# One fp32 transformer pair on one core: short vectors laid out as columns, x turned, the first w_ada sums moved ahead, and ScalarE copying both turned maps

## The reference, cut to what matters

```python
def first_block(x, c, ...):
    mod = silu(c) @ w_ada + b_ada              # 2048 -> 6 x 2048
    shift_a, scale_a, gate_a, shift_f, scale_f, gate_f = split(mod, 6)
    h = rms_norm(x, g_attn_pre) * (1 + scale_a) + shift_a
    proj = h @ w_in                            # 2048 -> 5456
    ...                                        # differential and indexed sparse attention
    x = x + gate_a * rms_norm(concat(diff_out, dsa_out) @ w_o, g_attn_post)
    h = rms_norm(x, g_ffn_pre) * (1 + scale_f) + shift_f
    x = x + gate_f * rms_norm((silu(h @ w_gate) * (h @ w_up)) @ w_down, g_ffn_post)

def second_block(x, ...):
    ...                                        # norm, w_in_2, 16 heads of MLA, a gated convolution, w_out_2
```

## Time and profile before

| what | before |
|---|---|
| median of 3 runs | 2403.71 us (2403.37 to 2404.49) |
| the profiled execution, its own time | 2403.83 us |
| its span from first to last instruction | 2402.5 us |
| TensorE busy, share of the span | 2288.5 us, 95% |
| VectorE busy | 1400.4 us, 58% |
| ScalarE busy | 1065.3 us, 44% |
| bytes moved | 505.69 MB, mean 210 GB/s |

### The profile page before, as it was taken

How to read it: one execution, slowest core, us unless ns; L and a number is a source line. 1 busy time by engine, 2 the same in 40 slices (tenths; PEclk the granted TensorE clock), 3 DMA queues, 4 the chain that set the end, 5 groups by cost and what they waited for, 6 DMA issues and landing times.

```text
span 2402.5 us, 26312 instructions
## 1 busy us (share of the span) xinstructions
PE 2288.5 (95%) x10768; PEld 1858.3 (77%) x10768; DVE 1400.4 (58%) x1903; ACT 1065.3 (44%) x1471; POOL 0.7 (0%) x5
## 2 busy tenths in 40 slices
PE   4899989889999999999998999999999999999998
PEld 2676767777888888888887878888888888888886
DVE  1459999795775464554456554545544554554554
ACT  2333544444444444434444555555444444444443
POOL 0000000000000000000000000000000000000000
PEclk7999999998999999999999999999999999999999
DMA  7888678593786675556553744444565555555553
GB/s 295 332 321 297 228 263 305 196 357 123 272 281 219 202 253 190 180 194 195 187 193 118 237 149 154 149 154 153 193 193 193 186 184 193 191 191 195 180 188 140
DMA packets 255455, 505.69 MB, mean 210 GB/s; under 512 B 9077, under 2 KB 19662, under 8 KB 254182
## 3 DMA queue, kind: packets, MB, share of 16 engines
q1 hardware_dynamic: 255334, 504.00, 62.2%
HBM read 499.77 MB, written 4.19 MB: 210 GB/s over the span
## 4 chain that ended last, share of the span: by engine, by line
PE 86%; DVE 7%; ACT 3%; DMA 2%; issue 1%; SPq 0%; DVEq 0%; ACTq 0%
PE bank L595 27%; PE bank L597 26%; PE bank L596 26%; DVE wlo L1674 2%; PE bank L611 2%; DMA raw<-in_w_in_dram 2%; DVE acc L1655 1%; PE bank L679 1%; ACT whi L1062 1%; DMA raw<-in_w_ada_dram 1%; PE bank L549 1%; PE bank L619 1%; DVE x L1726 0%; PE bank L702 0%; PE bank L531 0%
## 5 line engine op out<-in xcount | busy, mean ns | idle before, releaser
L1674 DVE TENSOR_TENSOR wlo<-raw,whi 128x1024 fp32r<-128x1024 f32 (+2 forms) x760 | 912.8, 1205 | 871.9 <-ACT whi L1062 870.2
L1062 ACT ACTIVATE whi<-raw 128x1024 fp32r<-128x1024 f32 (+2 forms) x760 | 789.9, 1044 | 1037.9 <-PE bank L597 917.5
L595 PE MATMUL bank<-whi,Ahi 128*128 128x512 f32 (+2 forms) x2304 | 910.8, 395 | 33.6 <-DVE wlo L1674 22.2
L596 PE MATMUL bank<-wlo,Ahi 128*128 128x512 f32 (+2 forms) x2304 | 896.6, 389 | 0.0
L597 PE MATMUL bank<-whi,Alo 128*128 128x512 f32 (+2 forms) x2304 | 896.4, 389 | 0.0
L595 PEld LDWEIGHTS bank<-whi,Ahi 128*128 128x128 f32 x2304 | 437.3, 190 | 132.9 <-DVE wlo L1674 31.9
L597 PEld LDWEIGHTS bank<-whi,Alo 128*128 128x128 f32 x2304 | 437.2, 190 | 90.2
L596 PEld LDWEIGHTS bank<-wlo,Ahi 128*128 128x128 f32 x2304 | 437.9, 190 | 83.4
L1655 DVE SCALAR_TENSOR_TENSOR acc<-raw,cs,acc 128x512 f32<-128x512 f32 x224 | 157.2, 745 | 0.1
L595 PE MATMUL bank<-whi,Fhi 128*128 128x512 f32 x352 | 137.6, 391 | 0.0
L597 PE MATMUL bank<-whi,Flo 128*128 128x512 f32 x352 | 137.1, 389 | 0.0
(11 more groups left out here) (291 smaller groups left out, 1344.3 us busy)
## 6 DMA issues: line engine op xcount, KB each, us to landing
raw<-in_w_in_dram SPq DMA_DIRECT2D x156, 1024.0 KB, 5.0
raw<-in_w_ada_dram SPq DMA_DIRECT2D x96, 1024.0 KB, 6.8
raw<-in_w_gate_dram SPq DMA_DIRECT2D x44, 1024.0 KB, 5.1
raw<-in_w_up_dram SPq DMA_DIRECT2D x44, 1024.0 KB, 5.1
raw<-in_w_down_dram SPq DMA_DIRECT2D x44, 1024.0 KB, 5.0
raw<-in_w_o_dram SPq DMA_DIRECT2D x16, 1024.0 KB, 6.7
raw<-in_w_o_mla_dram SPq DMA_DIRECT2D x16, 1024.0 KB, 4.9
raw<-in_w_o_conv_dram SPq DMA_DIRECT2D x16, 1024.0 KB, 4.9
```

The costliest lines, as they stand in the source:

```text
L595: pe.matmul(o, a_hi, w_hi, start=beg, stop=False)
L596: pe.matmul(o, a_hi, w_lo, start=False, stop=False)
L1062: act.activation(m.whi[:, i % NHL, :, 0:n], m.raw[:, c % NRAW, 2 * h:2 * h + 2, 0:n], ACT.Copy).then_inc(m.s_hi, 1)
L1674: dve.tensor_tensor(m.wlo[:, i % NHL, :, 0:n], m.raw[:, c % NRAW, 2 * h:2 * h + 2, 0:n], m.whi[:, i % NHL, :, 0:n].bitcast(F32), ALU.subtr ...
```

## The change

1. Short vectors, b_ada, positions, lambdas and x are laid out on the host: `columns` (128 x 121), `bias_columns` (128 x 96), `positions_both`, `lambdas`, and `x_turned` (columns of x on the partitions, 128 x 16 x 256). No arithmetic is done there. The ten small loads at the head become one; positions and lambdas become two loads that follow the ninth chunk.
2. x comes turned, so the mean squares are made over the partitions: ScalarE squares two halves, VectorE adds eight blocks of each (`red`), TensorE multiplies by ones, ScalarE takes the root, VectorE the reciprocal (`rstdT`). `turn_quarter` falls out of the first four quarters. VectorE makes `x * gs * rstdT` (`first_scale`), ScalarE adds the shift and rounds, VectorE makes the low part in one fused instruction (`first_shift`).
3. `first_scale` needs only the scale sums. They are made after the third chunk of a round, the shift's after the fourth. For the first quarter ScalarE's copies (`gather`) go ahead of the high parts of w_in, and the scale's sums stand among the products of the second group.
4. x in its plain form is loaded later, in four pieces, into the same space.
5. In sparse attention and MLA ScalarE copies both turned maps.

```diff
-    sp.dma_start(m.const[:, :], A["consts"]).then_inc(m.s_const, 16)
-    for r0, n, src in ((R_C, 16, A["c"][0]), ... (R_SUB, 1, A["g_diff_sub"][0])):
-        sp.dma_start(m.rows[r0:r0 + n, :], src.rearrange("(r n) -> r n", n=P)).then_inc(m.s_rows, 16)
...
+    sp.dma_start(m.cols[:, :], A["columns"]).then_inc(m.s_cols, 16)
+    load_chunk(0)
+    sp.dma_start(m.const[:, :], A["consts"]).then_inc(m.s_const, 16)
+    load_chunk(1)
+    for h in range(2):
+        sp.dma_start(m.xT[:, 8 * h:8 * h + 8, :], A["x_turned"][:, 8 * h:8 * h + 8, :]).then_inc(m.s_xT[h], 16)
+    load_chunk(2)
+    sp.dma_start(m.bT[:, :], A["bias_columns"]).then_inc(m.s_bT, 16)
+    for c in range(3, NRAW):
         load_chunk(c)
...
+        if c == LIN[0][0]:
+            sp.dma_start(m.pos[:, :], A["positions_both"]).then_inc(m.s_pos, 16)
+            sp.dma_start(m.lraw[:, :, :].rearrange("p a d -> p (a d)"),
+                         A["lambdas"].broadcast_to([P, 256])).then_inc(m.s_lamin, 16)
+        if c in at_x:
+            tb, h = divmod(at_x.index(c), 2)
+            need.wait_ge(m.s_shlo, 8)
+            cols = slice(1024 * h, 1024 * h + 1024)
+            sp.dma_start(x[:, tb, cols], A["x"][0, tb * P:tb * P + P, cols]).then_inc(m.s_x, 16)
```

TensorE:

```diff
+    def beside(idx, j):
+
+        if (idx, j) == (1, 0):
+            need.wait_ge(m.s_const, 16)
+            k.use(4)
+            for h in range(2):
+                need.wait_ge(m.s_red, h + 1)
+                ins = pe.matmul(m.bank[4][:, 0:S], m.ones, m.red[:, h, :], start=(h == 0), stop=(h == 1))
+            ins.then_inc(m.filled[4], 1)
+        if (idx, j) == (1, 2):
+            ada_columns(0)
...
-    ada_products(0)
-    first_operand(0)
+    ada_products(0, beside)
+    ada_columns(1)
     for q, cg in WIN_ITEMS[:3 * len(W_IN_FIRST)]:
         first_part(q, cg)
+        if cg == W_IN_FIRST[2]:
+            ada_columns(2 * q + 2)
         if cg == W_IN_FIRST[3]:
-            first_operand(q + 1)
+            ada_columns(2 * q + 3)
```

ScalarE (its squares, its shift, and both maps):

```diff
+    for h, o in enumerate((m.sq[:, :, :], m.tmpA[:, :, :, :].rearrange("p a k t -> p (a k) t"))):
+        need.wait_ge(m.s_xT[h], 16)
+        act.activation(o, m.xT[:, 8 * h:8 * h + 8, :], ACT.Square).then_inc(m.s_sq, 1)
+    warm_sqrt()
+    need.wait_ge(m.filled[4], k.use(4))
+    act.activation(m.rms[:, :], m.bank[4][:, 0:S], ACT.Sqrt, bias=m.eps[:, :], scale=1.0 / D).then_inc(m.freed[4], 1)
...
+                ins = act.activation(m.Ahi[:, kb, :], m.tmpA[:, q % 2, kk, :], ACT.Identity, bias=m.modT[:, kb:kb + 1])
...
     gather(0)
+    gather(1)
+    k.split_to(UNIT_AT[LIN[1]])
     first_operand(0)
...
-            copy_out(ln.ET[:, 0:384], b0, ex[0], m.bank[b0][:, 0:384])
+            for mm, b in enumerate(ln.bank[0:nm]):
+                copy_out(ln.ET[:, 384 * mm:384 * mm + 384], b, ex[mm], m.bank[b][:, 0:384])
...
-        copy_out(ln.ET[:, 0:384], 4, ex[0], m.bank[4][:, 0:384])
+        for mm in range(2):
+            copy_out(ln.ET[:, 384 * mm:384 * mm + 384], 4 + mm, ex[mm], m.bank[4 + mm][:, 0:384])
```

VectorE:

```diff
+        dve.tensor_reduce(m.red[:, h, :], i.rearrange("p k t -> p t k"), AX_X, ALU.add).then_inc(m.s_red, 1)
+    need.wait_ge(m.freed[4], k.use(4))
+    rstd_at = v.up(dve.reciprocal(m.rstdT[:, :], m.rms[:, :]))
...
+    def first_scale(q):
+
+        k.use(6)
+        mod(ADA_ON_PE[2 * q], 6, k.use(6))
...
+            ins = dve.scalar_tensor_tensor(out=m.tmpA[:, q % 2, kk, :], in0=m.xT[:, kb, :], scalar=m.gs[:, kb:kb + 1],
+                                           in1=m.rstdT[:, :], op0=ALU.mult, op1=ALU.mult)
...
+    def first_shift(q):
+
+        k.use(7)
+        mod(ADA_ON_PE[2 * q + 1], 7, k.use(7))
+        if q == 0:
+            k.split_to(UNIT_AT[LIN[1]])
...
+                ins = dve.scalar_tensor_tensor(out=m.Alo[:, kb, :], in0=m.tmpA[:, q % 2, kk, :],
+                                               scalar=m.modT[:, kb:kb + 1], in1=m.Ahi[:, kb, :].bitcast(F32),
+                                               op0=ALU.add, op1=ALU.subtract)
...
     for q, cg in WIN_ITEMS[:3 * len(W_IN_FIRST)]:
         first_part(q, cg)
         if cg == W_IN_FIRST[2]:
-            gather(q + 1)
+            first_scale(q + 1)
         if cg == W_IN_FIRST[3]:
-            first_operand(q + 1)
+            first_shift(q + 1)
         if (q, cg) == WIN_ITEMS[2]:
             tables()
...
-            if nm == 2:
-                need.wait_ge(m.filled[b1], ex[1])
-                dve.tensor_copy(ln.ET[:, 384:768], m.bank[b1][:, 0:384]).then_inc(m.freed[b1], 1)
```

More of the change, by code:

```diff
@@ L419, in __init__ @@
         after_P1 = shelf.top
-        self.rows = sb("rows", [P, P])
-        self.brows = sb("brows", [96, P])
         self.pos = sb("pos", [P, 4], I32)
@@ L536, in ada_take, with ada_products @@
             ins.then_inc(m.filled[b], 1)
-    def ada_products(c):
+    def ada_products(c, beside=None):
         while c < len(PLAN) and PLAN[c][0] == "ada" and c not in ADA_NO:
@@ L552, in ada_products @@
             c += 1
+            if beside:
+                beside(ADA_ON_PE.index(g), j)
     def ada_columns(idx):
@@ L1779, in shifted @@
             ins.then_inc(m.freed[b], 1)
-            if early:
-                low(j)
-        if not early:
-            low(0)
-            low(1)
-    def gather(q):
-        for idx in (2 * q, 2 * q + 1):
-            k.use(6 + idx % 2)
-    def first_operand(q):
-        for idx in (2 * q, 2 * q + 1):
-            b = 6 + idx % 2
-            mod(ADA_ON_PE[idx], b, k.use(b))
-        released(mod_at[4 + q], mod_at[q])
+            ks = slice(4 * q + 2 * j, 4 * q + 2 * j + 2)
+            need.wait_ge(m.s_shhi, base + 2 * q + j + 1)
+            dve.tensor_tensor(m.Alo[:, ks, :], tmp[:, q % 2, 2 * j:2 * j + 2, :], m.Ahi[:, ks, :].bitcast(F32),
+                              ALU.subtract).then_inc(m.s_shlo, 1)
+    def first_scale(q):
+        k.use(6)
+        mod(ADA_ON_PE[2 * q], 6, k.use(6))
+        released(mod_at[4 + q])
         ks = slice(4 * q, 4 * q + 4)
@@ L1798, in first_operand @@
         settle()
-        shifted(m.tmpA, q, 0, 0, False)
+        need.wait_ge(m.s_red, 2)
+        need.wait_ge(m.s_v, rstd_at)
+        if q > 1:
+            need.wait_ge(m.s_shlo, 2 * q - 2)
+        for kk in range(4):
+            kb = 4 * q + kk
+            ins = dve.scalar_tensor_tensor(out=m.tmpA[:, q % 2, kk, :], in0=m.xT[:, kb, :], scalar=m.gs[:, kb:kb + 1],
+                                           in1=m.rstdT[:, :], op0=ALU.mult, op1=ALU.mult)
+            if kk % 2 == 0:
+                v.up(ins)
+            else:
+                ins.then_inc(m.s_t, 1)
+    def first_shift(q):
[3 more added lines that the diff above has]
+            k.split_to(UNIT_AT[LIN[1]])
+        released(mod_at[q])
+        need.wait_ge(m.s_t, 2 * q + 2)
+        settle()
+        for j in range(2):
+            need.wait_ge(m.s_shhi, 2 * q + j + 1)
+            for kk in (2 * j, 2 * j + 1):
+                kb = 4 * q + kk
+                ins = dve.scalar_tensor_tensor(out=m.Alo[:, kb, :], in0=m.tmpA[:, q % 2, kk, :],
+                                               scalar=m.modT[:, kb:kb + 1], in1=m.Ahi[:, kb, :].bitcast(F32),
+                                               op0=ALU.add, op1=ALU.subtract)
+                if kk % 2 == 0:
+                    v.up(ins)
+            ins.then_inc(m.s_shlo, 1)
     part_at = {}
@@ L2136, in vector_program @@
     released(*y_at)
+    need.wait_ge(m.s_x, 64)
     for tb in range(2):
@@ L2550, in constants, with laid_out, rows @@
     return c
-_INS = ["x", "c", "positions", "w_ada", "b_ada", "g_attn_pre", "g_attn_post", "g_ffn_pre", "g_ffn_post", "w_in",
-        "lambda_q1", "lambda_k1", "lambda_q2", "lambda_k2", "g_diff_sub", "w_o", "w_gate", "w_up", "w_down",
-        "positions_2", "pre_norm_g_2", "w_in_2", "q_a_norm_g_2", "w_q_b_2", "kv_a_norm_g_2", "w_kv_b_2", "conv_w_2",
-        "w_o_mla_2", "w_o_conv_2", "w_out_2", "post_norm_g_2"]
+_INS = ["x", "w_ada", "b_ada", "g_attn_post", "g_ffn_post", "w_in", "w_o", "w_gate", "w_up", "w_down", "w_in_2",
+        "w_q_b_2", "w_kv_b_2", "w_o_mla_2", "w_o_conv_2", "w_out_2", "post_norm_g_2"]
+def laid_out(inputs):
+    def rows(name):
+        return np.asarray(inputs[name]).reshape(-1, P)
+    columns = ("c", "g_attn_pre", "g_ffn_pre", "pre_norm_g_2", "q_a_norm_g_2", "kv_a_norm_g_2", "conv_w_2", "g_diff_sub")
+    return {
+        "columns": np.concatenate([rows(n) for n in columns]).T,
+        "bias_columns": rows("b_ada").T,
+        "positions_both": np.concatenate([rows(n) for n in ("positions", "positions_2")]).T,
+        "lambdas": np.concatenate([np.asarray(inputs[n]) for n in ("lambda_q1", "lambda_k1", "lambda_q2", "lambda_k2")],
+                                  axis=1),
+        "x_turned": np.asarray(inputs["x"])[0].T.reshape(KD, P, S).transpose(1, 0, 2),
+        "consts": constants(),
+    }
 def kernel(**inputs):
@@ L2564 @@
     arrays, aps = {}, {}
-    for name in [*_INS, "consts"]:
```

(3 more changed lines are left out.)

136 lines of the change are left out of this document (46 added, 90 removed).

## The result

The changed kernel took **2381.95 us** (median of 4, 2381.28 to 2383.45), the kernel before, beside it, 2403.72 us (2403.37 to 2404.49): a ratio of 0.991, with an interval of [0.9893, 0.9927]. The forecast was 2382.0 us. The sum behind it was right in its two large terms and wrong in a smaller one, the rounds. That the two times agree so closely is luck: the same kernel taken again gave 2384.33 us.

A forecast was written before the change was run, and what follows sets the result against it. TensorE, busy 95% of the span, was taken as the bound, so a change counts only where it waits. Terms -10.0 - 2.8 - 1.2 - 1.0 - 6.7 = -21.7 from 2403.83 gave about 2382 us, range 2376 to 2393.

The forecast's parts named there:

- the rounds: Four rounds over quarters of w_in, 48.75 to about 177 us: net -1.2 us, bounds -5.3 and +3.
- The stream of loads: Kernel start: first w_ada chunk issued earlier, six small loads moved behind the ninth chunk; -10.0 us, bounds -7.1 and -10.8.
- The hole: Between w_ada's fifth and sixth chunk, behind six small loads: 7.1 us more than one chunk, forecast to close.
- From the last chunk to the first matmul: Start, last w_ada chunk to w_in's first matmul: 6.1 us instead of 8.84, -2.8 us, bounds -1.5 and -3.4.
- The reductions: Start, VectorE's two reductions of x's squares: 2.2 us each at 1.0 ns an element, 5.5 us spare before TensorE wants them.
- its point of 2.3 times: Strided-reductions rival at the start: beyond 2.3 times slower, each extra us holds TensorE's sixth chunk; 2416 us at ten times, chance 0.03.
- That stall: Rounds, before w_in's fifth chunk: TensorE waits 4.9 us for VectorE behind the rotation tables, 4.1 more than before.
- the third round ending some 14 us earlier: Sign that would show the forecast: the end of the third w_in round comes some 14 us earlier than before.
- The rival "loads set the rounds": Rounds wait for loads throughout, so only the stream's 10.0 us survives of the early terms: 2386 us, chance 0.12.
- Sparse attention: Before 470 us: four copies of 0.55 us move from VectorE to ScalarE; -1.0 us, bounds 0 and -2.2.
- MLA: MLA stage, 1380 to 1720 us: ScalarE's second copy lets TensorE go on 0.95 us earlier, seven times; -6.7 us.
- x read twice: Near 250 us: x loaded again in four 512 KB pieces, 1.3 us each; costs 0, bound +5.1.

The follow-up runs named there:

- the kernel with 16 matmuls more a round: Changed kernel plus 16 matmuls of 128x128 on the identity, results unused, in each of its first three rounds: 2388.91 us, ratio 0.9941.
- the first profile: First profiled execution of the unedited changed kernel, compared with the kernel before: 2383.45 us; the median of its runs was 2381.95 us.
- the five profiles with the changed kernel's rounds: Changed kernel twice, the two with MLA's or sparse attention's second copy back on VectorE, and one with two waits filled: rounds 124.2 to 128.5 us.
- the copies alone: Kernel before with only ScalarE copying both turned maps in sparse attention and MLA: 2393.57 us, ratio 0.9958.

## Why the prediction was right, step by step

- **The stream of loads, -10.0 us: right** (-9.65 at the eighth chunk's products). The hole did close. What made it I had left open; the runs put 4.2 us on the lambdas and 2.0 on the positions. Not all of it lasts: the first w_in chunk lands 9.6 us earlier than before (32.03 against 41.67), the second only 7.2 (44.76 against 51.92; 7.0 to 8.8 in the nine other profiles with the same order of loads). The new loads of positions and lambdas, which the forecast had put at nothing, stand right behind the first and cost 1.0 us there (0.7 to 2.0); where the rest goes was not looked into.
- **From the last chunk to the first matmul, 6.1 us forecast: right in size** (5.51; 5.5 to 7.0 in the other profiles with the same code and loads up to there). One cause was not in the working: before, TensorE stood 8.58 us ahead of the sixth chunk and its products ran at a granted clock of 0.50 up to the eighth. With a gap put back there by the old small loads, the changed code takes 8.3 us from the eighth chunk's landing too (33.71 to 40.90 from its products, all at 0.50), against 5.6 without and 8.9 before. So the new path is 3.3 us shorter where the clock stays up and 0.6 where it is down: part of this term's 2.8 us hangs on a condition that the forecast did not name.
- **The reductions, 2.2 us each: mis-sized.** They took 3.67, a factor of 1.67, and 2.9 us of the 5.5 spare were used up. The direction had been named as a rival, and its point of 2.3 times was not reached. The same shape read side by side, in the kernel with 16 matmuls more a round, took 2.28 us:

```profile
L2462 DVE TENSOR_REDUCE sg<-sg 128x256 f32<-128x2048 f32 x1 | 2.3, 2275 | 0.0
```

  So the forecast's 1.0 ns an element is nearly right for neighbours (1.1), and with steps of 1 KB it is 1.8. The Trainium skill, "SBUF — State Buffer", section "Door 1: The DMA port swizzle", says that an access that crosses to a new 16-byte line pays a penalty; this pair of rows agrees in direction. That the step between 16-byte lines is the cause, and not some other property of the step, was not tried.
- **The rounds, -1.2 us: the step that failed.** They gave 3.8 us back in the first profile. Over the five profiles with the changed kernel's rounds they are 126.0 us on average, against 124.7 and 121.7 in two profiles with the old rounds: some 2.8 us given back. The error was to credit the turning of x with its full 5.3 us of TensorE time, as if only the wait at the tables stood against it. That stall was right (5.39 us, 4.9 forecast). But the other waits of the rounds end 2.39 us after a load lands, whatever TensorE did before. With less work TensorE was idle longer, 16.8 us on average (14.4 to 18.3) instead of 11.2 and 11.1, which is 5.6 more where the forecast had 4.1, and its busy time fell by 2.9 us instead of 5.3, as the mean granted clock was 0.90 to 0.93 against 0.93 and 0.96. Of work put back, less than half shows (5 of 11 us). The sign named for this, the third round ending some 14 us earlier, did not come in the first profile: it is 9.2 us at unit 28, and 13.0 in the second. The rival "loads set the rounds" had the mechanism for all waits but the one at the tables; its 2386 us did not come. Why the clock was lower stays open.
- **Sparse attention, -1.0 us: right** at 0.8 (0.5 with the copies alone), though the first profile showed 2.3. Reading that as the copy's would have been wrong.
- **MLA, -6.7 us: right** at 6.8, in every profile. The wait per pair is 4.1 / 7 = 0.59 us on average (0.4 forecast), 0.39 in the pair shown.
- **x read twice, 0: right.** The four loads go out from 242.8 to 266.1 us. Units 30 to 62 hold their shift of 9.2 us within 0.06, and units 64 to 83 stand at 9.4 to 9.5, so nothing was lost.
- **Not in the sum:** the clock at the start of the feed-forward, 1.7 us for the changed kernel in the first profile and 0.4 against it in the second.

The first profile had the long rounds and, against them, the short forms of units 90 and 120; so the terms of that profile were off by 5.0 us one way (the rounds) and 3.7 the other (sparse attention 1.3, the start of the feed-forward 1.7, the small rest 0.7), and its own time of 2383.45 us is 1.3 over what the sum gives from the profile before, 2382.1. That the median met it within 0.1 us is chance. All nine runs of the changed kernel average 2383.2 us.

## What to carry to other kernels

Where a stage waits for one short operation again and again on a full engine, count the waits and move it: that forecast was good to 0.1 us in 6.7. Where loads and an engine wait for each other in turn, find out with a dose experiment what work taken off the engine is worth, since here less than half of it showed. Before a gain of 1 to 2 us is put down to an edit, look at the same stretch in an unedited run.

## What the hardware showed that I had not expected

- **The clock behind a wait is a matter of the run.** Two waits of 2.4 to 2.5 us stand ahead of units 88 and 90, 9 us apart. Behind one or both of them the clock falls to 0.50 and comes back. (Where it stays up behind the first, the second wait is longer, 4.00 us in the kernel with MLA's copy on VectorE, as TensorE comes earlier.) In the same kernel it fell behind the first alone in one profile and behind both in another: 4.69 and 6.20 us for the unit behind the second wait.

```profile
417.61:422.30 4.69, 4.69 (x30) 4.20 (x31) 4.22 (x6) 1.64 (x4) 0.00 (x0) 1.00 1.01 386
```

```profile
413.86:420.06 6.20, 6.20 (x31) 5.31 (x31) 4.22 (x6) 1.64 (x4) 0.00 (x0) 0.74 0.96 342
```

  A fall behind the first wait costs nothing: the way from unit 88 to unit 90 takes 11.41 us with it (the changed kernel) and 11.42 at a full clock (the kernel with MLA's copy on VectorE), since VectorE ends the second wait either way.
- **A matmul that does nothing can be worth its time.** 9.54 us of them in a wait of 10.4 kept the clock at 1.00 and saved 0.9 to 3.0 us in the stretch behind it.
- **Four broadcast loads of 32 KB each held the stream of 1 MB loads back by 4.2 us**; as one load of 128 KB they land 0.9 us behind the load ahead of them (32.20 and 33.08 us), and the next chunk 2.6 us later. Together with the positions' load they cost the stream 1.0 us there, against 6.2 for all the old loads.
